# Where the fourth stage's shift is multiplied, and when two groups of modulation blocks are loaded, in a two-block transformer kernel

## The reference, cut to what matters

```
shift, scale, gate = split(silu(c) @ w_mod + b_mod)       # per stage
h = norm(x) * (1 + scale) + shift
x = x + gate * stage(h)                                   # second block
```

## Time and profile before

| | before |
|---|---|
| median of three runs | 2184.05 us |
| the profiled execution, its time | 2176.38 us |
| its span | 2174.6 us |
| mean granted TensorE clock | 0.951 |
| TensorE busy | 1988.9 us |
| VectorE busy | 1693.8 us |
| ScalarE busy | 1164.1 us |
| read from HBM | 551.40 MB, 254 GB/s over the span |

### The profile page before, as it was taken

How to read it: one execution, slowest core, us unless ns; L and a number is a source line. 1 busy time by engine, 2 the same in 40 slices (tenths; PEclk the granted TensorE clock), 3 DMA queues, 4 the chain that set the end, 5 groups by cost and what they waited for, 6 DMA issues and landing times.

```text
span 2174.6 us, 28297 instructions
## 1 busy us (share of the span) xinstructions
PE 1988.9 (91%) x11530; PEld 1719.2 (79%) x11530; DVE 1693.8 (78%) x1781; ACT 1164.1 (54%) x1270; POOL 72.9 (3%) x121
## 2 busy tenths in 40 slices
PE   6878999878889999999999999868789999979999
PEld 6666898777568887888788788667679998858998
DVE  6675888877588889899899988887778897676444
ACT  3543334464367776777777777544543445544432
POOL 6001000000100000000000000000010000000000
PEclk9988999989899999999999999978889999988999
DMA  9743799832389999999999999935229995323552
GB/s 354 239 165 136 267 335 369 287 129 97 136 294 331 349 367 362 331 354 375 333 347 359 370 335 351 325 111 200 97 85 338 353 369 175 114 78 117 180 188 97
DMA packets 251208, 554.37 MB, mean 255 GB/s; under 512 B 10076, under 2 KB 75856, under 8 KB 251072
## 3 DMA queue, kind: packets, MB, share of 16 engines
q1 hardware_dynamic: 247252, 544.13, 70.2%
q0 software_dynamic: 3552, 8.29, 1.1%
q10 hardware_dynamic: 268, 0.07, 0.0%
HBM read 551.40 MB, written 1.05 MB: 254 GB/s over the span
## 4 chain that ended last, share of the span: by engine, by line
PE 68%; DVE 16%; ACT 7%; DMA 4%; issue 4%; SPq 0%; ACTq 0%; DVEq 0%
PE bank L491 21%; PE bank L492 20%; PE bank L493 20%; DVE ring_lo L1905 4%; ACT ring_hi L1244 3%; DMA ring<-in_w_in_dram 2%; PE bank L880 1%; DMA ring<-in_ffn_w_dram 1%; DVE acc L1845 1%; DMA ring<-in_ada_w_dram 1%; PE bank L1069 1%; DVE work L2088 1%; DVE XN L2141 1%; ACT work L1370 1%; PE bank L573 1%
## 5 line engine op out<-in xcount | busy, mean ns | idle before, releaser
L1905 DVE TENSOR_TENSOR ring_lo<-ring,ring_hi 128x2048 fp32r<-128x2048 f32 x417 | 950.3, 2287 | 252.6 <-ACT ring_hi L1244 249.9
L1244 ACT ACTIVATE ring_hi<-ring 128x2048 fp32r<-128x2048 f32 x417 | 795.5, 1913 | 488.5 <-PE bank L493 235.8
L491 PE MATMUL bank<-hh,ring_hi 128*128 128x256 f32 x1152 | 333.6, 290 | 20.4 <-ACT QK L1434 8.8
L492 PE MATMUL bank<-hl,ring_hi 128*128 128x256 f32 x1152 | 331.6, 288 | 0.0
L493 PE MATMUL bank<-hh,ring_lo 128*128 128x256 f32 x1152 | 331.2, 287 | 0.0
L491 PE MATMUL bank<-ring_hi,hh 128*128 128x256 f32 (+2 forms) x672 | 218.1, 325 | 34.9 <-ACT PT L1384 10.3
L491 PEld LDWEIGHTS bank<-hh,ring_hi 128*128 128x128 f32 x1152 | 227.1, 197 | 25.2 <-issue 14.0
L493 PE MATMUL bank<-ring_hi,hl 128*128 128x256 f32 (+2 forms) x768 | 243.4, 317 | 0.0
L491 PE MATMUL bank<-ring_hi,hgh 128*128 128x512 f32 (+1 forms) x576 | 220.3, 382 | 8.8 <-DVE ring_lo L1905 3.6
L492 PEld LDWEIGHTS bank<-hl,ring_hi 128*128 128x128 f32 x1152 | 227.0, 197 | 0.7 <-issue 0.2
L493 PEld LDWEIGHTS bank<-hh,ring_lo 128*128 128x128 f32 x1152 | 226.9, 197 | 0.0
(11 more groups left out here) (418 smaller groups left out, 2781.9 us busy)
## 6 DMA issues: line engine op xcount, KB each, us to landing
ring<-in_moe_w_dram SPq DMA_DIRECT2D x264, 1024.0 KB, 5.2
ring<-in_ada_w_dram SPq DMA_DIRECT2D x48, 1024.0 KB, 7.3
ring<-in_w_mod_dram SPq DMA_DIRECT2D x48, 1024.0 KB, 7.3
ring<-in_w_in_dram SPq DMA_DIRECT2D x40, 1024.0 KB, 5.9
ring<-in_ffn_w_dram SPq DMA_DIRECT2D x33, 1024.0 KB, 5.6
ring<-in_w_gate_dram SPq DMA_DIRECT2D x22, 1024.0 KB, 5.1
ring<-in_w_up_dram SPq DMA_DIRECT2D x22, 1024.0 KB, 5.0
ring<-in_w_down_dram SPq DMA_DIRECT2D x22, 1024.0 KB, 5.0
```

The source lines that it names most:

```text
L491: pe.matmul(ps, xh, wh, start=first, stop=False)
L492: pe.matmul(ps, xh, wl, start=False, stop=False)
L1244: act.activation(ring_hi[i % NH][:, 0:z], ring[n % NS][:, 0:z], ACT.Copy).then_inc(*s.hi(("hi", home(s, i), i)))
L1905: dve.tensor_tensor(ring_lo[n % NS][:, 0:z], ring[n % NS][:, 0:z], hi, ALU.subtract).then_inc(*s.lo(("lo", home(s, i), i)))
```

## The change

- The four blocks of (4, 0) leave the first feed-forward, which keeps 28 modulation blocks. They are loaded behind the last block of the experts, ahead of `win2` block 0.
- They are multiplied by TensorE: `ON_PE` has them, so VectorE skips them. TensorE does the four products after the drain, ahead of `to_features`, and then adds the bias with eight matmuls of one column (`bias_sum`, new).
- The four blocks of (4, 2) leave the experts and join the eight of (5, 0) and (5, 1) between the 12 `win2` blocks of stage 4.
- (4, 1) stays where it was, four blocks earlier in count. The order in which the first accumulator is used changes from 0, 1, 4, 3, 5, 7 to 0, 1, 3, 4, 5, 7, and the bias loads on GpSimd follow: (4, 0) is prepared with (4, 2).

```diff
-            order = [0, 1, 4, 3, 5, 7] if j < 2 else [0, 1, 2, 3, 4, 5, 7]
+            order = [[0, 1, 3, 4, 5, 7], [0, 1, 4, 3, 5, 7], [0, 1, 2, 3, 4, 5, 7]][j]
...
-        ON_PE = [("mod", 0, 0, 0), ("mod", 0, 1, 0)] + [("mod", 0, 2, p) for p in range(4)]
+        ON_PE = [("mod", 0, 0, 0), ("mod", 0, 1, 0)] + [("mod", m, j, p) for m, j in ((0, 2), (4, 0)) for p in range(4)]
...
-                         mods((1, 2), (4, 0), (4, 1), (2, 0), (2, 1), (2, 2), (3, 0), (3, 1))))
+                         mods((1, 2), (4, 1), (2, 0), (2, 1), (2, 2), (3, 0), (3, 1))))
...
-        put_blocks(weave(ffn_blocks(*[(("moe", x), a["moe_w1"][0, x], a["moe_w3"][0, x], a["moe_w2"][0, x]) for x in range(8)]), mods((4, 2)), 6, 6))
-        IN_MOE = [(4, 2)]
+        put_blocks(ffn_blocks(*[(("moe", x), a["moe_w1"][0, x], a["moe_w3"][0, x], a["moe_w2"][0, x]) for x in range(8)]))
+        put_blocks(mods((4, 0)))
...
-            put_blocks(weave(win2, mods((5, 0), (5, 1)) if l == 0 else []) + rowblocks(("wout2", l), a["w_out_2"][l]))
+            put_blocks(weave(win2, mods((4, 2), (5, 0), (5, 1)) if l == 0 else []) + rowblocks(("wout2", l), a["w_out_2"][l]))
...
+            def bias_sum(m, j):
+
+                pe.wait_ge(*at("bias", m, j))
+                for i in range(8):
+                    x = pe.matmul(Y[0][j][:, i:i + 1], acc_of(j)[:, 128 * i:128 * i + 128], ones[:, 0:1], start=False, stop=i == 7)
+                x.then_inc(*main.small(("sum", m, j)))
...
                 if l:
                     together(m)
                 else:
-                    summed((m, "start"))
+                    for p in range(4):
+                        gemv(("mod", 4, 0, p))
+                    bias_sum(4, 0)
                 to_features(("h", m), XN, [[("n", m, 0)], [("n", m, 1)]])
...
-            bias(4, 0, 1)
+            bias(4, 1)
             bias(2, 0, 1, 2)
...
-            bias(4, 2)
+            bias(4, 0, 2)
```

More of the change, by code:

```diff
@@ L394, in hybrid_kernel @@
                     need, place = turn_of[END[m]], (m, "end")
-                if m == 4 or (m == 3 and j == 2):
+                if (m, j) in ((4, 1), (3, 2)):
                     need, place = moe0, (3, "router")
-                if (m, j) in IN_MOE:
-                    i, need = moe1 + 4, len(split)
+                if (m, j) == (4, 0):
+                    i, need = len(split), 0
                 sums.setdefault(i if i < need else place, []).append((m, j))
@@ L546, in summed @@
                 for m, j in sums.get(place, []):
-                    if (m, j) == (0, 2):
+                    if (m, j) in ((0, 2), (4, 0)):
                         continue
@@ L1892, in columns_of @@
                     x = dve.scalar_tensor_tensor(cols[:, m, 8:16], ps[:, 0:8], 1.0, pB[:, c:c + 8], ALU.add, ALU.mult)
-                x.then_inc(*vec(("cols", m, j)))
+                x.then_inc(*vec(("cols", m, j), *([("cols", 4, 1)] if (m, j) == (4, 0) else [])))
             def low_halves(s, upto):
```

## The result

The kernel after takes 2190.16 us, the median of 12 runs (2183.82 to 2198.42). The kernel before, run beside it on the same chip, takes 2181.16 us (12 runs, 2174.85 to 2185.84). The ratio is 1.004, with a 95% interval of 1.0029 to 1.0052; the medians lie 9.0 us apart, after is slower. The profiled execution of after took 2189.97 us, with a span of 2188.2.

A forecast was written before the change was run, and what follows sets the result against it. Bound by DMA in the first feed-forward, TensorE among the experts, VectorE and ScalarE in the passage, VectorE in early stage 4. -11.1 - 4.0 + 18.3 + 5.5 = +8.7 us on 2180.2 gives 2188.9; range 2171 to 2203.

The forecast's parts named there:

- Step 1: First feed-forward, four blocks fewer: 11.1 us faster, with TensorE idle only 2 to 3 us.
- lower bound of 8.8: First feed-forward: smallest gain, from the 3.70 us at the end, half of the remaining idle, and the sum.
- Rival 3: First feed-forward gets no faster, its blocks waiting for buffer order and not DMA: +18 us in all, 2198; chance 0.07.
- Step 2: Experts, four blocks fewer: 4.0 us faster, from TensorE's waits for `ring_lo` behind the blocks.
- the bound of -5.1: Experts: largest gain, counting one block's 2.60 us in full in place of the first 1.15 us wait.
- Step 3: Passage to stage 4: four products and a bias sum on TensorE at clock 0.50, 18.3 us slower.
- Rival 1: Passage: the clock rises under the one-column matmuls, so -0.6 us there and -10.2 in all, 2170; chance 0.12.
- Step 4: Stage 4, four more blocks on VectorE: 5.5 us slower, bounds 2.6 and 10.3.
- the point at 92.8 us: Stage 4: what the prediction called the first product of attention's values, reached after 92.8 us with eight blocks.
- The two idle times: Stage 4: VectorE's waits of 2.75 us at 1449.63 and 1.63 at 1524.88, into which one block of each pair falls.
- By pairs: Stage 4: two extra blocks ahead of the first scores, 2.6 us, and two behind them, 1.8 + 1.1.
- Rival 2: Stage 4: VectorE's chain takes all four blocks, +10.3 in place of +5.5, +15.8 in all, 2196; chance 0.14.

The follow-up runs named there:

- e2_shift: The kernel after with (4, 2) put back among the experts, so only (4, 0) is moved; 2186.95 us, ratio 1.0019 against before.
- e6_experts: The kernel after, but (4, 0) and (4, 2) both stand among the experts, multiplied by VectorE; 2176.78 us, ratio 0.9978 against before.
- the last three: e10_pool, e11_bank and e12_early, built on e6_experts; 2178.57, 2178.39 and 2172.95 us.
- e1_gate: The kernel before with only the (4, 2) blocks moved from the experts to stage 4; 2186.32 us, ratio 1.0024 against before.
- e9_late: e1_gate with the (4, 2) blocks between the row blocks at the end of stage 4; 2189.16 us, ratio 1.003 against before.
- e5_burst: The kernel after plus 20 dummy 512-column products on TensorE behind the drain, ahead of the (4, 0) products; 2185.61 us, ratio 1.0011 against before.
- e12_early: e11_bank, but GpSimd sets up the (5, 0) accumulator once TensorE has turned the features; 2172.95 us, ratio 0.9953 against before.
- e5_mixed: e5_burst plus one dummy 512-column product behind every second one-column matmul of (4, 0); 2200.84 us, ratio 1.0087 against before.
- e10_pool: e6_experts, but GpSimd sets up the (5, 0) accumulator only after project(0) of stage 4; 2178.57 us, ratio 0.9976 against before.
- e11_bank: e10_pool, but TensorE sums (4, 0) into a bank of its own; 2178.39 us, ratio 0.9978 against before.

## Why the prediction was right, and where it was not

The forecast was +8.7 us and 2189; measured are +9.0 and 2190.2. It holds by sign and size, and by mechanism in its first three terms. The fourth, stage 4, was too small by a third, and the others made up for half of that; that the total came out within 0.3 us is in part luck.

**Step 1, first feed-forward: forecast -11.1.** Over the nine experiments with the same list there as after (e2_shift to e6_experts and the last three) the stage takes 197.5 to 199.4 us, 198.2 in the mean, a gain of 10.4 on the 208.6 of before and e1_gate (e9_late, with the list of before, took 211.0). The term was right (-11.1 with the sum's 1.75), though its lower bound of 8.8 does not follow from its parts: 3.70, half of the remaining 5.6, and 1.75 are 8.25. The sign was right too where nothing disturbs it. Counted from the stage's first product, TensorE idles 9.4 us in before and 1.5 to 2.7 in those nine, against the 2 to 3 that I named.

After's own execution gave only 7.2 us, and TensorE idles 4.5 us in it. The largest wait within the stage is

```profile
222.31 0.38 PE L491 MATMUL bank<-hh,ring_hi 128*128 128x256 f32 x1 [2.01 <-DVE ring_lo L1915]
```

and the clock is at 0.50 from 223.3 to 226.8 behind it; another wait for `ring_lo`, of 1.39 us, stands at 254.5. Since the other kernels have the same list, I take this for one execution's bad luck; it was not tested further. ScalarE's waits for blocks in this stage went from 108.2 us over 28 only to this:

```profile
ACT ring_hi L1253 <- DMA ring<-in_ffn_w_dram: 97.6, 27, 10.1
```

So the sum of such a wait is no measure of what TensorE loses by it. Rival 3, that nothing is gained there, is refuted.

**Step 2, experts: forecast -4.0.** Measured -4.6 to -5.6 in the kernels without a block there (822.5 to 823.5 against 828.1). TensorE's waits for `ring_lo` in that stage fell from 10.6 us in all to 7.2, which is 3.4 and close to the 3.65 that I added up; but they are not all that the blocks cost, and the bound of -5.1 was the better value. Where the rest stood was not followed.

**Step 3, the passage: forecast +18.3.** Measured +17.3 in after and +17.8 in e2_shift. Each part of the working is in the trace: the level 0.50 (0.51 with the first moments), products and sum 30.2 us (1400.34 to 1430.51) against the 30.8 forecast, transposes 3.65 against 3.6, and 1.6 from there to the first product against 2.0. From VectorE's first norm row to the first product it is 35.4 us against 18.1 before; I had named 36 to 37. The reason, that these matmuls run at the lower level and neither raise it nor keep it, had been read from one opening and one short sum; after and e5_burst show it in the passage itself. Rival 1 is refuted there. The opening was the weaker witness: in eight of the thirteen traces made later the level did rise there, at 20 to 22 us, when TensorE was at the end of its first 32 one-column instructions and 16 transposes of 128 columns. It fell again under the next one-column matmuls (e2_shift: up at 20.8, down at 24.2, with TensorE busy from 21.9 on).

**Step 4, stage 4: forecast +5.5. This is the term that was mis-sized.** Measured +8.2 in after and +8.8 in e1_gate, which has nothing else: 2.1 us a block, not 1.4. By parts, from the first product of the stage: the first scores come at 52.4 against 47.8 us, the first product of values at 71.4 against 65.1 (the point at 92.8 us that the prediction called so is a later one), the first `yT` at 120.4 against 112.0, the end at 179.2 against 171.0. In e1_gate the same four stand at 51.0, 70.9, 120.3 and 179.8.

VectorE does the same work in the same order in all three traces, but for the four extra blocks. So one can match it row by row and see where the delay against before grows. In after:

```profile
1451.95 1.22 DVE L2377 TENSOR_REDUCE st<-XN 128x16 f32<-128x1024 f32 x1 [0.85 <-ACT XN L1573]
...
1466.08 2.29 DVE L1915 TENSOR_TENSOR ring_lo<-ring,ring_hi 128x2048 fp32r<-128x2048 f32 x1 [0.88 <-ACT ring_hi L1253]
...
1477.29 2.60 DVE L1854 SCALAR_TENSOR_TENSOR acc<-ring,csil,acc 128x1024 f32<-128x1024 f32 x2 [0.47 <-DVE acc L1854]
...
1532.56 2.60 DVE L1854 SCALAR_TENSOR_TENSOR acc<-ring,csil,acc 128x1024 f32<-128x1024 f32 x2
1535.08 2.28 DVE L1915 TENSOR_TENSOR ring_lo<-ring,ring_hi 128x2048 fp32r<-128x2048 f32 x1
```

| where VectorE's delay grows | after | e1_gate |
|---|---|---|
| first extra block, up to the row at 1451.95 | +0.5 | -0.5 |
| new wait for ScalarE, at 1466.08 | +1.0 | +1.0 |
| second block, at 1477.29 | +3.1 | +2.7 |
| small waits around the scores | +0.3 | +1.2 |
| third block, 67.7 and 67.2 us into the stage | +2.7 | +2.7 |
| fourth block, at 1532.56 | +0.8 | +0.8 |
| from there to the end | -0.2 | +0.9 |
| together | +8.2 | +8.8 |

The two idle times on which I had counted did their part. The wait of 2.75 us at 1449.63 shrank to 0.85 in after and to nothing in e1_gate, and took up most of the first block or all of it. The one of 1.63 us at 1524.88 is gone: no wait stands ahead of the row at 1535.08, and the fourth block cost 0.8. The two other blocks counted in full, and the second of after waits another 0.47 us for the block ahead of it. By pairs, I had 2.6 for the first and 1.8 + 1.1 = 2.9 for the second; measured are 3.6 and 3.5 in after, 2.2 and 3.5 in e1_gate. The waits that make the rest, 1.1 in after and 3.1 in e1_gate, I had at nothing. The largest of them that both have is the one for ScalarE at 1466.08. ScalarE is late there because its own block is:

```profile
1464.13 1.92 ACT L1253 ACTIVATE ring_hi<-ring 128x2048 fp32r<-128x2048 f32 x1 [6.38 <-DMA ring<-in_w_in_dram]
```

SyncE issued that block at 1456.40, 0.4 us behind a modulation block, and it released ScalarE 7.7 us later; in e1_gate the same took 7.9 us. In before it was issued at 1453.66, 0.4 us ahead of a modulation block, and released ScalarE at 1458.70, 5.0 us later. So the extra blocks seem to cost something in the DMA queue too, beside VectorE's time; no run separates the two. Rival 2, all four at 10.3, is refuted by the first and the fourth block; the size of its term was as near as mine.

The four terms as measured are -10.4 (the mean of nine), -5.1, +17.3 and +8.2, in all +10.0, against +9.0 by the medians.

## What to carry to other kernels

Price a piece of work at each place where it could stand, by the wait that ends last there. Here a block of 1 MB cost about 2.6 us in the first feed-forward (the last four of 32, where TensorE waited for blocks; the four below them next to nothing), 1.3 among the experts while there were up to eight, 2.6 from there on, 2.1 in the mixer, and on TensorE in the passage nothing for the first 13 us of products and sum, and then 6.7 a block (32 instructions x 0.209). The cheapest place was one that the change was leaving, and it pays in full only once what hangs on the moved work (the memset, the bank of the sum, the bias load) has been placed too: the same block list gave -4.8 us in e6_experts and -10.3 in e12_early, and the trace of the second shows where: 3.0 us in the passage, from the memset and the bank.

## What the runs showed of the hardware

- One-column fp32 matmuls kept TensorE busy, but not its clock up. At the lower level they did not raise it in 30 us without a gap (after, 1400.34 to 1430.51). Started at the upper level in e5_burst, with TensorE busy ahead of them and all through them, they lost it at 1407.7 and did not get it back before they ended; it rose at 1435.0, behind 16 transposes of 128 columns. One full product of 512 columns to every two such matmuls did not keep it either (e5_mixed, 0.50 from 1405.8).
- A GpSimd memset of 128 x 1024 fp32 beside VectorE's TENSOR_SCALAR of the same size lengthened the latter from 0.81 to 1.65 us (e6_experts against e10_pool), though GpSimd is busy for 3% of the span only.
- A bias of 4 KB, loaded among block loads, was usable 5.5 us after GpSimd issued it (e11_bank). A whole block of 1 MB, the one issued at 1453.66 in before, took 5.0 us.
